# Where the causal and window masks of the wide score units are added in a hybrid SSD and sparse-attention layer

## What is computed

```python
def nsa_attend(q, q_pos, kv_c, kv_s, kv_w, kw_pos):        # 128 queries at a time, 8 heads of 64, 2 KV heads
    sc = einsum(q, kv_c[K]) * scale                        # 32 block means, "c"
    ...
    ss = einsum(q, chosen 64-key blocks[K]) * scale        # "s": top 16 of 16 blocks, so every key up to the query
    ms = (tok <= q_pos)
    ps = masked_softmax(ss, ms)
    sw = einsum(q, kv_w[K]) * scale                        # "w": window of 512 keys behind the query
    mw = (dist >= 0) & (dist <= WINDOW)
    pw = masked_softmax(sw, mw)
    # masked_softmax: s = where(mask, s, -inf); m = max(s); e = exp(s - m); e / sum(e)
```

## Time and profile before

| | us |
|---|---|
| runs | 924.77, 924.91, 926.18 |
| median | 924.91 |
| span of the profiled execution | 928.3 |
| PE matmuls busy in it | 864.5 |
| DVE busy in it | 454.6 |
| ACT busy in it | 354.5 |

### The profile page before, as it was taken

The page is one execution under the profiler, slowest core; times in us unless marked ns, Lnnn a source line. Parts: engine busy times, 40 slices in busy tenths (PEclk is TensorE's granted clock), DMA queues, the critical chain, the costliest instruction groups (busy, mean ns, idle before and its releaser), DMA issues. The chain is left out here.

```text
span 928.3 us, 19131 instructions
## 1 busy us (share of the span) xinstructions
PE 864.5 (93%) x8245; PEld 504.4 (54%) x8245; DVE 454.6 (49%) x838; ACT 354.5 (38%) x714; POOL 201.4 (22%) x174
## 2 busy tenths in 40 slices
PE   2999999999999999999899998789999999899887
PEld 1454674455566656667555555445646464654553
DVE  1133031052535244447654536887876867567511
ACT  3041000210201034554333236775665656454523
POOL 1001765000200033334410110137211130303021
PEclk9999999999999989999999999899999999999989
DMA  8937137322220000020843452710011010202102
GB/s 280 354 114 278 64 126 248 156 91 90 91 93 0 1 5 1 19 73 1 305 159 119 163 164 41 231 61 23 14 47 49 13 60 5 68 3 69 60 2 90
DMA packets 44461, 88.98 MB, mean 96 GB/s; under 512 B 4196, under 2 KB 25900, under 8 KB 43034
## 3 DMA queue, kind: packets, MB, share of 16 engines
q1 hardware_dynamic: 39354, 56.02, 18.5%
q0 software_dynamic: 5024, 31.75, 9.4%
HBM read 75.49 MB, written 16.40 MB: 99 GB/s over the span
## 5 line engine op out<-in xcount | busy, mean ns | idle before, releaser
L1778 PE MATMUL PS<-hT,W 128*128 128x363 f32 (+1 forms) x384 | 118.6, 469 | 0.0
L1758 PE MATMUL PS<-W,hT 128*128 128x512 f32 x256 | 113.3, 595 | 0.5 <-DVE W L1421 0.5
L1576 DVE TENSOR_REDUCE small<-PS 128x1 f32<-128x640 f32 (+7 forms) x86 | 82.6, 968 | 52.0 <-PE PS L2104 50.3
L1778 PEld LDWEIGHTS PS<-hT,W 128*128 128x128 f32 x384 | 72.2, 189 | 45.6 <-issue 1.7
L1708 PE MATMUL PS<-W,hT 128*128 128x288 f32 (+1 forms) x256 | 86.5, 500 | 0.0
L1758 PEld LDWEIGHTS PS<-W,hT 128*128 128x128 f32 x256 | 48.1, 191 | 57.1 <-issue 55.7
L878 POOL TENSOR_TENSOR Q<-Q,U 128x512 f32<-128x512 f32 x16 | 20.3, 1269 | 267.1 <-DVE U L1609 267.1
L1708 PEld LDWEIGHTS PS<-W,hT 128*128 128x128 f32 x256 | 48.5, 190 | 37.4 <-issue 30.7
L1147 ACT ACTIVATE hT<-PS,small 128x128 f32<-128x128 f32 (+7 forms) x64 | 47.0, 741 | 51.6 <-DVE small L1576 51.5
L2054 PE MATMUL PS<-U,Y 128*128 128x512 f32 x128 | 60.4, 603 | 0.8 <-ACT OTb L1154 0.8
L2054 PE MATMUL PS<-U,Q 128*128 128x512 f32 x128 | 59.3, 599 | 0.0
(11 more groups left out here) (457 smaller groups left out, 1557.2 us busy)
## 6 DMA issues: line engine op xcount, KB each, us to landing
W<-in_w_in SPq DMA_DIRECT2D x5, 2048.0 KB, 8.8
W<-in_w_ada SPq DMA_DIRECT2D x8, 1024.0 KB, 10.4
U<-in_x_prompt SPq DMA_DIRECT2D x8, 512.0 KB, 7.7
W<-in_w_ada SPq DMA_DIRECT2D x2, 2048.0 KB, 8.0
U<-in_state_win_kv POOLq DMA_DIRECT2D x8, 512.0 KB, 5.1
W<-in_x_prompt SPq DMA_DIRECT2D x8, 512.0 KB, 3.3
out_y_prompt<-W SPq DMA_DIRECT2D x8, 512.0 KB, 2.7
out_new_win_sample<-in_state_win_kv POOLq DMA_DIRECT2D x1, 4032.0 KB, 24.0
```

What stands on the lines that cost most here:

```text
L1576: nc.vector.tensor_reduce(sneg_m[u % 2][:, 0:nh], scores(u), AX.X, ALU.max, negate=True).then_inc(s_max, 1)
L1758: ins = nc.tensor.matmul(bank(z_bank(u)), hT3[:, k, i * P:(i + 1) * P], w, start=(k == 0), stop=(k == KT8 - 1))
L1778: ins = nc.tensor.matmul(bank(b, 0, n), w[:, k, ct % 4 * P:ct % 4 * P + P], hT3[:, k, a:a + n], start=(k == 0), stop=(k == KT8 - 1))
```

## The change

The step MASK is taken out of the order, and with it its 128 bf16 matmuls (48 at L2101 and L2103, 80 at L2104). The last score matmul of a wide unit now ends its accumulation and tells DVE. In SOFTMAX of a wide unit DVE first adds the mask in place in PSUM: for a unit with an edge one addition over the first 128 columns and one over the last 128, for the others one over the last 128 (of both heads at once in a unit of two heads). It then waits for its own last addition (`link`) and takes the row maximum as before. The masks are read in fp32 from the constants. The bf16 copy of the edge mask goes, with its 128 columns. The order is otherwise the same, letter for letter. Units of more than two heads keep their mask matmul.

```diff
-        masks = sb("masks", 4 * P, BF16)
+        masks = sb("masks", 3 * P, BF16)
@@
-        identb, edgeb, clearb, causb = (masks[:, n * P:(n + 1) * P] for n in range(4))
+        identb, clearb, causb = (masks[:, n * P:(n + 1) * P] for n in range(3))
@@ (ORDER: every letter d is taken out, the rest is unchanged; first and last lines)
-            "qqssxsdxydxwmtsvcdxtqksdysxdvxcszsxdxwkgddsdtmstxdvvcsdaxykuwsxtmootodoogaxtoooqtssdrrdvxppvctxtskudsvdxtpvxsdvc"
+            "qqssxsxyxwmtsvcxtqksysxvxcszsxxwkgstmstxvvcsaxykuwsxtmootooogaxtoooqtssrrvxppvctxtskusvxtpvxsvc"
...
-            "vtstvxdxvvctkuvvnvvvcokoooorogoauofrooonhofroooornhf")
+            "vtstvxxvvctkuvvnvvvcokoooorogoauofrooonhofroooornhf")
@@ (DVE, constants)
-            nc.vector.memset(clearb, 0.0)
-            link(nc.vector.tensor_copy(edgeb, const("edge")))
+            link(nc.vector.memset(clearb, 0.0))
@@ (DVE, SOFTMAX)
                         if u >= 2:
                             dve.wait_ge(s_exp, u - 1)
+                        if nh <= 2:
+                            for at, mask in ((0, const("edge")), (n * P - P, const("caus")))[0 if has_edge(u) else 1:]:
+                                x = scores(u)[:, :, at:at + P]
+                                ins = nc.vector.tensor_tensor(x, x, mask.unsqueeze(1).broadcast_to([P, nh, P]), ALU.add)
+                            link(ins)
                         nc.vector.tensor_reduce(sneg_m[u % 2][:, 0:nh], scores(u), AX.X, ALU.max, negate=True).then_inc(s_max, 1)
@@ (PE, S)
-                            if nh > 2:
-                                stop = x == nh // 2 - 1
-                            else:
-                                stop = nh == 1 and half == 0 and not has_edge(u)
+                            stop = nh <= 2 or x == nh // 2 - 1
                             ins = nc.tensor.matmul(PS[:, base + c:base + c + m], QD[i % 2][HALF[half], hh, :], keys_on(half, k, i, hh // GQ, lo, m),
                                                    start=nh <= 2, stop=stop)
-                    if nh > 2:
-                        ins.then_inc(s_scores, 1)
-                elif what == "MASK":
-                    i, k, h, nh = UNITS[u]
-                    if k == "c" or nh > 2:
-                        continue
-                    first, second = (u % 2 * 1024 + parts[0][3] for parts in score_parts(u))
-                    m = score_parts(u)[0][0][2]
-                    if has_edge(u):
-                        nc.tensor.matmul(PS[:, first:first + P], identb, edgeb, start=False, stop=True)
-                    if nh == 2:
-                        nc.tensor.matmul(PS[:, first + m - P:first + m], identb, causb, start=False, stop=True)
-                    nc.tensor.matmul(PS[:, second + m - P:second + m], identb, causb, start=False, stop=True).then_inc(s_scores, 1)
+                    ins.then_inc(s_scores, 1)
```

More of the change, by code:

```diff
@@ L611, in build_layer @@
         OUTPUT = ("GATE", "SCALE", "TURN", "OUT", "RES", "SQUARE", "ROOT", "FINAL")
-        NAMES = {"q": "QT", "z": "SAMPLE", "s": "S", "d": "MASK", "x": "SOFTMAX", "t": "TURNP", "y": "CT", "w": "CV", "v": "PV", "k": "BACK",
+        NAMES = {"q": "QT", "z": "SAMPLE", "s": "S", "x": "SOFTMAX", "t": "TURNP", "y": "CT", "w": "CV", "v": "PV", "k": "BACK",
                  "c": "COPY", "m": "SUM", "g": "GATE", "a": "SCALE", "u": "TURN", "o": "OUT", "r": "RES", "n": "SQUARE", "h": "ROOT", "f": "FINAL",
@@ L617, in build_layer @@
         ORDER = (
-            "qqssxsdxydxwmtsvcdxtqksdysxdvxcszsxdxwkgddsdtmstxdvvcsdaxykuwsxtmootodoogaxtoooqtssdrrdvxppvctxtskudsvdxtpvxsdvc"
[L619 to L622, removed]
-            "vtstvxdxvvctkuvvnvvvcokoooorogoauofrooonhofroooornhf")
+            "qqssxsxyxwmtsvcxtqksysxvxcszsxxwkgstmstxvvcsaxykuwsxtmootooogaxtoooqtssrrvxppvctxtskusvxtpvxsvc"
+            "sxoxspsotppxpoxqpkttsnsyorxoogxottosrvvvttcxsknxavsvvvcstxtuwsxxoqsstmkoxxftosstxoxossgoxtxooyrs"
+            "rvxvssfvtvxcaxstxwmkussxxvvststvvxxvsscxqkxosxtosnsoyxosxtstooxwxssrtgoxxossmrxvvxvsastvvtcx"
+            "xkussvvxxtnsxvssfxvsxxsxvyvsstcoxxqwossmotoxosxgstttoxroxaokssrnxvvxvsstvvctxxkussfxvvtvsxvs"
+            "xvxvvssctooxtsxgtxsoxorkssxvvvxsxvvcatytssoxouoxoftrssoxkoooxsnsrwtxoxossgomxxorasxvvstsvvfx"
+            "vtstvxxvvctkuvvnvvvcokoooorogoauofrooonhofroooornhf")
         VALUE_TILES = [min(u // 2, WIN // P if u % 2 else TT) + 1 for u in range(2 * TT)]
@@ L2082, in _ @@
                             o = PS[:, base + x * 512:base + x * 512 + nh // 2 * step].rearrange("p (h s) -> p h s", s=step)
-                            nc.tensor.matmul(o, identb, masks[:, 4 * P - step:].unsqueeze(1).broadcast_to([P, nh // 2, step]), start=True, stop=False)
+                            nc.tensor.matmul(o, identb, masks[:, 3 * P - step:].unsqueeze(1).broadcast_to([P, nh // 2, step]), start=True, stop=False)
                     for x, pair in enumerate(zip(*score_parts(u))):
                         for half, (hh, lo, m, c) in enumerate(pair):
-                            if nh > 2:
-                                stop = x == nh // 2 - 1
-                            else:
-                                stop = nh == 1 and half == 0 and not has_edge(u)
+                            stop = nh <= 2 or x == nh // 2 - 1
                             ins = nc.tensor.matmul(PS[:, base + c:base + c + m], QD[i % 2][HALF[half], hh, :], keys_on(half, k, i, hh // GQ, lo, m),
                                                    start=nh <= 2, stop=stop)
-                    if nh > 2:
-                        ins.then_inc(s_scores, 1)
-                elif what == "MASK":
-                    i, k, h, nh = UNITS[u]
-                    if k == "c" or nh > 2:
-                        continue
-                    first, second = (u % 2 * 1024 + parts[0][3] for parts in score_parts(u))
-                    m = score_parts(u)[0][0][2]
-                    if has_edge(u):
-                        nc.tensor.matmul(PS[:, first:first + P], identb, edgeb, start=False, stop=True)
-                    if nh == 2:
-                        nc.tensor.matmul(PS[:, first + m - P:first + m], identb, causb, start=False, stop=True)
-                    nc.tensor.matmul(PS[:, second + m - P:second + m], identb, causb, start=False, stop=True).then_inc(s_scores, 1)
+                    ins.then_inc(s_scores, 1)
                 elif what == "CV":
```

## The result

The changed kernel took 932.12 us (median of 20 runs), the kernel before 927.55 us (20 runs): a ratio of 1.0058, 95% interval 1.0039 to 1.0077. The profiled execution of the changed kernel spans 933.1 us against 928.3.

The account below looks back on a forecast made before the run. PE's own stream was taken to bound the stage. PE's gain of 9.7 us less 4.1 us of new waits gave -5.6 us, so 919.3 us on the median of 924.91; range 914 to 928.

Parts of the forecast that it names:

- The stage goes at the pace of PE's own stream: Stage from about 600 to 876 us: PE's own stream sets the pace for 260 of 276 us.
- PE gets back 9.7 us: Removing 128 mask matmuls from PE in the stage saves 9.7 us, between 7.3 and 11.5.
- 35.3 us on DVE: 112 mask additions ahead of DVE's row maxima add 35.3 us, going into 76.5 us of idle time.
- New waits 4.1 us: DVE lateness in tiles 2, 4 and 5 2.0 us, PE's gain not to be had 1.8, late RES 0.3.
- The sign to look for: PE's waits for the exponentials (L1147) up from 3 us to about 7, in tiles 2, 4 and 5.
- Rival 2: DVE becomes the bound from tiles 2 to 4, from about 0.5 us an addition; about 930 us; chance 0.15.
- Rival 3: PE's gain eaten by 9 to 10 us of new waits at S, perhaps lower clock; about 924.5 us; chance 0.15.
- three marks by which the prediction would have called itself wrong: Additions of 0.4 us or more; PE's OUT and PV starts keeping their distance without masks; over 10 us waiting for L1147.

Follow-up runs that it names:

- thinner PV: One of PV's four groups of 32 keys left out: in the kernel before 906.37 us, in that without masks 899.85, in the changed one 911.77.
- borders moved by half a block: 64 products of 8 columns added ahead of tile 1's branch c: kernel before 1.0134 and 1.0096, without masks 1.0040, changed kernel 1.0044.
- the shifts: Kernel before with 32, 64 or 96 extra products of 8 columns ahead of tile 1's branch c: 1.0052, 1.0096 (earlier 1.0134), 1.0063.
- four places: Kernel before and changed kernel with 0, 32, 64 and 96 extra products: changed less before +0.58%, -0.52%, -0.52%, +0.11%.
- steady burst: Kernel before with its first PV step done 25 times in place of once: 974.93 us, ratio 1.0522.

## Why the prediction was wrong, by its own steps

*"The stage goes at the pace of PE's own stream."* This step failed. The prediction saw 8.0 us of waits without a releaser and passed them over as held by nothing that is traced. They were the mark of the second limit of this stage, the arrival of instructions. The queue that brings them is in the trace, and the list of waits named the place: PV, the step with the most instructions per us. In its place the runs show PE's saving turned into standing: with the masks off PE alone 8.9 us less work and 8.0 us more standing, the waits without a releaser up from 9.4 to 16.3 us.

*"PE gets back 9.7 us."* The size is borne out (8.9 us less work on PE), but not that what PE saves can be had. Measured for the masks off PE alone: 0.8 us slower, within its interval of none. With thinner PV 6.5 us are gained, with the borders moved by half a block 5 to 9. A reading that fits, and that no run shows by itself: while a mask product ran, the next block came nearer; without it PE arrives at the border sooner and waits there. The run with masks of 8 columns shows it most plainly: 4.5 us off the masks, 4.7 us more in PV.

*"35.3 us on DVE."* Right: 0.289 us and 0.415 us an addition, against the 0.291 and 0.42 taken from the earlier trace rows. Writing PSUM in place cost what writing SBUF cost. The busy time of DVE in the stage rose by 27.1 us and not by 35: the 35 hold the waits for its own result (80 x 0.04), and the records of a pair of additions overlap (0.47 to 0.50 us for two). DVE's idle time ahead of the maxima fell to 23.0 us, forecast some 20.

*"New waits 4.1 us."* Right in size: the additions alone cost 4.1 us by the ratio. The waits behind that price are not so near: in that run those for other engines rose by 2.5 us. And the price hangs on the rest: 4.8 us between the kernel without masks and the changed one, 11.9 us with thinner PV, 0.4 us with borders moved by half a block (1.0044 against 1.0040, which these runs can't tell from 4). The sign to look for, PE's waits for L1147, was forecast at 7 us and is 2.8 + 1.5 + 0.6 = 4.9.

*The rivals.* Rival 2 had the sign and nearly the time (930), not the mechanism: the additions are far from the 0.5 us at which it decides, and DVE is idle for 49 us of the stage. The rule of the Trainium skill that led there (Perfetto Trace Analysis, Identifying the Most-Contended Engine) was right that the busy time of matmuls hides room on PE; it names DVE as the engine to relieve, and DVE's added work did cost some 4 us, but the gain was lost on PE by itself. Rival 3 had the size of what was lost: it put new waits at 9 to 10 us, and 25.6 - 16.4 = 9.2 came. It placed them at S, and 6.2 of them are waits for instructions. It alone named the clock, for which the forecast's sum has no term, and the changed kernel's clock did fall, from 0.986 to 0.978. Of the three marks by which the prediction would have called itself wrong, one came true in the sum of the stage: MASK, S, PV and OUT together took 281.3 us before, and S, PV and OUT without masks take 283.4. The other two did not (0.289 us an addition, 4.9 us of waits for L1147).

*What stays open.* How the +4.6 us splits between the additions, the place of the borders and the clock is not settled: with the same PE instructions the additions cost from 0.4 to 11.9 us, the shifts alone move the kernel before by 0.5 to 1.3%, and by the estimate above most of the difference between the timed runs goes together with the clock. Why the clock fell is open too. All kernels with a whole PV in which none of these mask products is left, or only a shrunk one, ran at 0.978 to 0.982, and all of them have longer waits without a releaser than the kernel before; but the kernel before with 64 products has 17.2 us of such waits and 0.983, and no run separates the two. Settled is that the changed kernel is slower at its own borders, that PE's saving turned into standing there, and that over four places the change is worth nothing that can be measured.

## What to carry to other kernels

Waits of PE that no engine ends, inside a run of small matmuls, can be a limit and no noise: count instructions per us there, and see whether each wait ends at the same distance behind a transfer of the instruction queue (here 1.2 to 1.6 us). Work taken off PE beside such a run was worth nothing here, so test the saving by itself first, with the work simply left out. Compare the granted clock of the timed runs as well as their times. And an edit of under 1% in a kernel like this is judged at several positions of its instruction blocks, for some dozens of idle products can move it as far as the edit.

## What the hardware did that was not expected

- A block of 256 PE instructions took 4.0 us to be replaced in a steady burst, with the other engines still; PV alone would use it up in 2.08 us. The stop of 1.92 us is ended 1.3 to 1.5 us behind the end of a 16 KB transfer that lasts 0.9 to 1.4 us. At half the clock (0.50) the block took PE 2.97 us, the stop was 1.03, and the 4.0 us stayed.
- Runs of the same kernel with a mean granted clock lower by 0.01 were 6.3 us longer, of some 930.
- 64 products of 8 columns, 1.6 us, cost 9 to 12 us at one place of the kernel before (1.0096 and 1.0134) and some 3 us at the same place of the kernel without masks (1.0040 against 1.0006).
- An addition that reads and writes PSUM in place takes 0.289 us for 128 columns and 0.415 us for 256, as much as one into SBUF.
